# A chunked delta-rule and forgetting-attention block: the filling projections of its last stage as pairs of 64-row products

## What is computed

```python
h = rmsnorm(x, norm_w)                       # 1024 tokens x 1024
proj = h @ w_in                              # gdn q/k/v/z/beta/alpha, fox q/k/v/z/f, 2048 gate logits
y_a = gated_deltanet(...)                    # 8 heads of 64, chunks of 64
y_b = forgetting_attention(...)              # 8 heads of 64, 128-query blocks:
#   s = q k^T / 8 + c_t - c_s  (s <= t);  softmax(s) @ v;  rmsnorm, times silu(z)
g_a, g_b = split(sigmoid(gate_logit + gate_b))
merged = g_a * (y_a @ w_up_gdn) + g_b * (y_b @ w_up_fox)
out = rmsnorm(x + merged @ w_out)
```

## Time and profile before

| | us |
|---|---|
| median of 3 runs | 946.38 (946.35 to 946.46) |
| the profiled execution | 946.32 |
| its span, first to last instruction | 944.5 |
| TensorE busy | 924.9 (98%) |
| VectorE busy | 610.3 (65%) |
| ScalarE busy | 473.1 (50%) |

### The profile page before, as it was taken

The page is one execution under the profiler, slowest core; times in us unless marked ns, Lnnn a source line. Parts: engine busy times, 40 slices in busy tenths (PEclk is TensorE's granted clock), DMA queues, the critical chain, the costliest instruction groups (busy, mean ns, idle before and its releaser), DMA issues.

```text
span 944.5 us, 15969 instructions
## 1 busy us (share of the span) xinstructions
PE 924.9 (98%) x6404; PEld 702.3 (74%) x6404; DVE 610.3 (65%) x983; ACT 473.1 (50%) x846; POOL 19.9 (2%) x29
## 2 busy tenths in 40 slices
PE   5999999999999999999999999999999999999997
PEld 5778787888888876676766666666667888888886
DVE  6487668799999934464496786767863433246252
ACT  7555654632866625532756547556554442334132
POOL 1000002020000000000000000000000000000000
PEclk9999999999999999999999999999999999999999
DMA  7111351249323393322553325234125323123162
GB/s 249 47 49 45 98 177 48 69 145 229 96 90 106 107 272 87 102 75 90 139 182 98 105 101 168 102 101 123 34 69 178 113 66 90 55 112 112 41 192 79
DMA packets 114704, 104.87 MB, mean 111 GB/s; under 512 B 33152, under 2 KB 94720, under 8 KB 114248
## 3 DMA queue, kind: packets, MB, share of 16 engines
q1 hardware_dynamic: 103256, 81.05, 30.4%
q10 hardware_dynamic: 10224, 18.62, 5.3%
q0 software_dynamic: 1152, 4.19, 1.4%
HBM read 76.84 MB, written 27.00 MB: 110 GB/s over the span
## 4 chain that ended last, share of the span: by engine, by line
PE 45%; DVE 3%; ACT 1%; DMA 1%; issue 1%; SPq 0%; DVEq 0%; ACTq 0%
PE pj L2287 6%; PE pj L2289 5%; PE pj L2288 5%; PE pc L2420 4%; PE pa L2386 3%; PE pa L2355 1%; PE pj L2298 1%; PE pj L2299 1%; PE pj L2300 1%; PE pj L2558 1%; PE pj L2556 1%; PE pj L2557 1%; PE pb L2446 1%; PE pb L2435 1%; PE pb L2557 1%; PE pb L2556 1%
## 5 line engine op out<-in xcount | busy, mean ns | idle before, releaser
L145 PE MATMUL pj<-h_hi,w_hi 128*128 128x512 f32 x504 | 203.6, 404 | 0.5 <-DVE w_lo L133 0.5
L146 PE MATMUL pj<-h_lo,w_hi 128*128 128x512 f32 x504 | 196.9, 391 | 0.0
L147 PE MATMUL pj<-h_hi,w_lo 128*128 128x512 f32 x504 | 196.5, 390 | 0.0
L145 PEld LDWEIGHTS pj<-h_hi,w_hi 128*128 128x128 f32 x504 | 94.5, 188 | 23.9 <-issue 1.1
L147 PEld LDWEIGHTS pj<-h_hi,w_lo 128*128 128x128 f32 x504 | 94.6, 188 | 20.4
L146 PEld LDWEIGHTS pj<-h_lo,w_hi 128*128 128x128 f32 x504 | 94.7, 188 | 17.9 <-issue 0.2
L2287 PE MATMUL pj<-h_hi,w_hi 128*128 128x512 f32 x248 | 101.3, 408 | 0.3 <-PEq L323 0.3
L2289 PE MATMUL pj<-h_hi,w_lo 128*128 128x512 f32 x248 | 96.8, 390 | 0.0
L2288 PE MATMUL pj<-h_lo,w_hi 128*128 128x512 f32 x248 | 96.7, 390 | 0.0
L2287 PEld LDWEIGHTS pj<-h_hi,w_hi 128*128 128x128 f32 x248 | 46.5, 188 | 19.5 <-issue 10.1
L598 ACT ACTIVATE xc<-pj 128x512 f32<-128x512 f32 x39 | 23.3, 597 | 72.2 <-PE pj L147 71.6
(11 more groups left out here) (372 smaller groups left out, 1867.9 us busy)
## 6 DMA issues: line engine op xcount, KB each, us to landing
w_raw<-in_w_in SPq DMA_DIRECT2D x48, 512.0 KB, 4.4
fox_scratch<-xc ACTq DMA_DIRECT2D x39, 256.0 KB, 2.8
qkv<-in_x SPq DMA_DIRECT2D x8, 512.0 KB, 6.4
fa<-rows_scratch POOLq DMA_DIRECT2D x8, 512.0 KB, 4.9
rv<-fr_scratch SPq DMA_DIRECT2D x16, 256.0 KB, 4.0
ma<-m_scratch SPq DMA_DIRECT2D x8, 512.0 KB, 3.9
rv<-in_w_out SPq DMA_DIRECT2D x8, 512.0 KB, 3.6
w_raw<-in_x SPq DMA_DIRECT2D x8, 512.0 KB, 4.4
```

The source lines that it names most:

```text
L145: nc.tensor.matmul(o, w_hi[:, slot, k], h_hi[:, k, cols], start=(k == 0), stop=False)
L146: nc.tensor.matmul(o, w_hi[:, slot, k], h_lo[:, k, cols], start=False, stop=False)
L147: last = nc.tensor.matmul(o, w_lo[:, slot, k], h_hi[:, k, cols], start=False, stop=(k == KT - 1))
```

## The change

From the second part of tile 1 on, the fills of tiles 1 to 7 are no longer products of 128 rows. `both_halves` gives TensorE each product as two of 64 rows, one for each half of the contraction rows, at the same time for different token halves: rows 0 to 63 add to half 0's bank while rows 64 to 127 add to half 1's (phase 0), and in phase 1 the other way round. `phase_done` holds phase 1 back until the banks of phase 0 are written. A fill is now a group of 24 such products (`fill()`), ten for each pair of heads, at the steps in `GROUP_STEP`: four groups for a gate tile, two for its up projection.

So both halves of a tile end at the same time. Both banks of `pj` hold gates and then both hold ups; there is a second pair of buffers `gate_r` and `mst_r`, and the up weights have one buffer for tiles 0 to 8. The two exponentials of a tile stand behind each other at one step, the two `plus` and `sigmoid` at the next. The first gate group of a tile waits for both `gated` of the tile before, the first up group for both exponentials. `gated` moves ahead in VectorE's steps. The up weights of tile 1, which were loaded beside tile 0's and split before the loop, are loaded and split at its start; the gate of tile 1's second half, still of 128 rows, is the first filling. Tile 9's up weights are split one round later.

```diff
-        up_hi = sb("up_hi", [P, 2, PAIRS, P], F32R, where=st)
-        up_lo = sb("up_lo", [P, 2, PAIRS, P], F32R, where=st)
+        up_hi_a = sb("up_hi_a", [P, PAIRS, P], F32R, where=st)
+        up_lo_a = sb("up_lo_a", [P, PAIRS, P], F32R, where=st)
+        with ExitStack() as own_gates:
+            gate_r = sb("gate_r", [P, HALF], where=own_gates)
+            mst_r = sb("mst_r", [P, HALF], where=own_gates)
+        up_hi_b = sb("up_hi_b", [P, PAIRS, P], F32R, where=st)
+        up_lo_b = sb("up_lo_b", [P, PAIRS, P], F32R, where=st)
...
-        gate_b1, mst_b1 = fa[:, 5, 0:HALF], fa[:, 6, 0:HALF]
+        gate_of, mst_of = (gate[:, :], gate_r[:, :]), (mst[:, :], mst_r[:, :])
+        up_hi = lambda tile: (up_hi_b if tile > KT and tile % 2 else up_hi_a)[:, :, :]
+        up_lo = lambda tile: (up_lo_b if tile > KT and tile % 2 else up_lo_a)[:, :, :]
...
-        AHEAD = 32
-        FILLS = ((8,) + (4,) * 4 + (0, 4) * 4) * PAIRS + (5, 4, 4, 3)
-        UNIT = KT + PAIRS
-        A_FILLS = KT * 2 * UNIT
+        GROUPS = 10
+        GROUP_STEP = (0, 0, 1, 2, 3, 4, 6, 8, 10, 12)
+        GATE_END = [None, 1] + [7 + 6 * t for t in range(KT - 2)]
+        UP_END = [None, 3] + [9 + 6 * t for t in range(KT - 2)]
...
-                    if tile > 1:
+                    if tile:
                         sp.wait_ge(up_ready, tile)
                     col = (tile % KT) * P
                     for b in range(2):
                         to = half_rows(1 - b if tile < KT else b)
-                        sp.dma_start((up_side if tile == 1 else up_raw)[to],
-                                     up_view[tile // KT][half_rows(b), :, col:col + P]).then_inc(
-                                         ma_loaded[0] if tile == 1 else up_loaded, 16)
+                        sp.dma_start(up_raw[to], up_view[tile // KT][half_rows(b), :, col:col + P]).then_inc(up_loaded, 16)
...
-                load_up(1)
...
-                load_up(2)
+                load_up(1)
                 for g in range(STEPS + TAIL):
                     p, s = divmod(g, PER)
                     v = s - 1
@@ -1563,6 +1558,8 @@
                     if v == 0 and p:
                         sp.wait_ge(u_step, 4 * p - 1)
                         load_fox(fz, 3, p, fz_loaded)
+                    if g == 1:
+                        load_up(2)
...
-                    if tile == 1:
-                        act.wait_ge(ma_loaded[0], SIDE)
-                    else:
-                        act.wait_ge(up_loaded, 32 * max(tile, 1))
-                    if tile >= 2:
+                    act.wait_ge(up_loaded, 32 * tile + 32)
+                    if 1 <= tile <= KT:
+                        act.wait_ge(up_done, 2 * tile)
+                    elif tile == KT + 1:
+                        act.wait_ge(up_free, 2 * KT)
+                        act.wait_ge(m_stored, 16 * 2 * KT)
+                    elif tile:
                         act.wait_ge(up_done, 2 * (tile - 1))
-                    nc.scalar.activation(up_hi[:, tile % 2], up_source(tile), ACT.Copy).then_inc(up_hi_done, 1)
+                    nc.scalar.activation(up_hi(tile), up_raw[:, :, :], ACT.Copy).then_inc(up_hi_done, 1)
...
-                    act.wait_ge(up_free, 1 if v == 2 else v)
-                    gate_exp(v, pj[:, 0], gate[:, :])
+                    if v >= 2:
+                        act.wait_ge(up_free, v - 1 if v < 4 else 2 * (v // 2))
+                    gate_exp(v, pj[:, v % 2], gate_of[v % 2])
...
                 exp_a(2)
+                split_up_hi(1)
                 store_m(1)
...
-                        split_up_hi(t + 2)
+                        split_up_hi(t + 1)
                     for u in gates_through(g):
                         exp_a(u)
...
-                def gated(v, buf, dst):
+                def gated(v):
                     dve.wait_ge(gate_act, 2 * v + 2)
-                    dve.wait_ge(up_done, v + 1)
+                    dve.wait_ge(up_done, 2 * (v // 2) + 2 if v >= 2 else v + 1)
                     if v == 0:
                         dve.wait_ge(const_made, 6)
-                    if v != 1:
-                        dve.wait_ge(m_stored, 16 * v)
-                    nc.vector.tensor_tensor(dst, pv_bank if v == 1 else pj[:, 1], buf, ALU.mult).then_inc(up_free, 1)
+                    if v >= 2:
+                        dve.wait_ge(m_stored, 16 * 2 * (v // 2))
+                    up = (pj[:, 1], pv_bank)[v] if v < 2 else pj[:, v % 2]
+                    nc.vector.tensor_tensor(mst_of[v % 2], up, gate_of[v % 2], ALU.mult).then_inc(up_free, 1)
...
-                split_up_lo(1)
...
-                        split_up_lo(t + 2)
+                        split_up_lo(t + 1)
...
-                        gated_steps(g)
                     elif s == 0:
                         if p:
                             low_part(p, 0)
                         row_max(p, 0)
                         if p == 0:
-                            gated(1, gate_b1, mst_b1)
+                            gated(1)
+                            split_up_lo(1)
                         row_max(p, 1)
                         row_max(p, 2)
                         row_max(p, 3)
                         low_part(p, 1)
-                        gated_steps(g)
                         spread_max(p, 0)
                         plus_steps(g)
                         gate_steps(g)
                     elif v < 4:
                         if v < 2:
                             row_max(p, 4 + 2 * v)
+                        if v > 1:
+                            add_weights(p, v - 1)
+                        gated_steps(g)
                         if v < 3:
                             plus_steps(g)
-                        if v > 1:
-                            add_weights(p, v - 1)
                         row_max(p, 5 + 2 * v)
                         if v == 3:
                             plus_steps(g)
@@ -2141,7 +2139,6 @@
                             out_gate(p - 1, 1)
                             add_squares(2 * p - 1)
                         gate_steps(g)
...
+                def both_halves(w, src, k, phase, first, last, done_sem, turns):
+
+                    for m, (w_part, s_part) in enumerate(((w[0], src[0]), (w[0], src[1]), (w[1], src[0]))):
+                        for r in range(2):
+                            half = r ^ phase
+                            ins = nc.tensor.matmul(pj[:, half], w_part[half_rows(r)], s_part[half_rows(r), k, half_cols(half)],
+                                                   start=(first and m == 0), stop=(last and m == 2))
+                            if last and m == 2:
+                                ins.then_inc(done_sem, 1)
+                            if turns and m == 2:
+                                ins.then_inc(phase_done, 1)
+
+                def gate_group(tile, c):
+
+                    slot = (N3 + tile) % 2
+                    if c == 0:
+                        pe.wait_ge(w_ready, N3 + tile + 1)
+                        pe.wait_ge(up_free, 2 * tile)
+                    phase = c // 2
+                    if c == 2:
+                        pe.wait_ge(phase_done, 4 * tile - 4)
+                    for k in range(4 * (c % 2), 4 * (c % 2) + 4):
+                        both_halves((w_hi[:, slot, k], w_lo[:, slot, k]), (h_hi, h_lo), k, phase,
+                                    phase == 0 and k == 0, phase == 1 and k == KT - 1, pj_done, phase == 0 and k == KT - 1)
+
+                def up_group(tile, phase):
+
+                    if phase == 0:
+                        pe.wait_ge(up_ready, tile + 1)
+                        pe.wait_ge(pj_free, 2 * N3 + 2 * tile + 4)
+                    else:
+                        pe.wait_ge(phase_done, 4 * tile - 2)
+                    for k in range(PAIRS):
+                        both_halves((up_hi(tile)[:, k], up_lo(tile)[:, k]), (ya_hi, ya_lo), k, phase,
+                                    phase == 0 and k == 0, phase == 1 and k == PAIRS - 1, up_done, phase == 0 and k == PAIRS - 1)
+
+                def fill():
+
+                    n = done[0]
+                    done[0] += 1
+                    if n < 2:
+                        for k in range(4 * n, 4 * n + 4):
+                            gate_product(3, k)
+                    elif n < 4:
+                        up_group(1, n - 2)
+                    else:
+                        tile, c = 2 + (n - 4) // 6, (n - 4) % 6
+                        if c < 4:
+                            gate_group(tile, c)
+                        else:
+                            up_group(tile, c - 4)
...
                         weight_sums(p - 1, 1)
                     max_scores(p, 0)
                     max_scores(p, 1)
-                    fill(3)
+                    fill()
                     max_scores(p, 2)
                     turn_values(p, 0)
                     max_scores(p, 3)
-                    fill(5)
+                    fill()
```

118 lines of the change are left out of this document (49 added, 69 removed).

## The result

The changed kernel takes 962.8 us, median of four runs (962.1 to 963.5), against 946.4 us of the kernel before, run beside it (four runs, 946.35 to 948.75). The ratio is 1.0163, with a 95% interval of 1.0146 to 1.0179. It is slower, as forecast, by 16.4 us where 11.7 were expected. The profiled execution took 963.3 us, with a span of 961.5.

What follows compares the result with a forecast made beforehand. TensorE, busy 924.9 of 944.5 us at full clock, was taken as the bound. 946.32 - 7.4 (shape changes) + 1.6 (pairs) + 10.2 (start waits) + 7.3 (later waits) = 958.0 us; forecast 954 to 962, range 946 to 964.

Steps and rivals of the forecast that it cites:

- rival 3: More waits of the later kind, 1.5 to 2 us for each of seven tiles: 12 instead of 7.3, time 963; chance 0.07.
- (c): Pair 0, step 1: ScalarE must split tile 3's late-loaded gate weights before slot 1's exponentials; TensorE's piece 8 waits 4.0 us.
- TensorE's own row: 39 fewer changes of shape at 0.19 us save 7.4 us, 456 pairs add 1.6: 5.8 us won.
- (a): Start of pair 0: VectorE's split of tile 1's late-loaded up weights delays piece 3 by 4.1 us, `turn_max` by 0.7.
- (b): Start of pair 0: exponential of tile 1's second half stands behind a sigmoid and weight split on ScalarE; 1.4 us.
- Tiles 4 and 5's gates: First gate groups in pairs 1 and 2 wait for both `gated` of the tile before: 1.85 and 2.1 us.
- step 9: Pairs 0 and 3: two sigmoids and a weight split ahead of slot 9's exponentials delay slot 11's scores, 0.65 us each.
- Slot 7 of pair 2: Two sigmoids and a weight split go ahead of slot 5's exponentials, whose bank slot 7 needs: TensorE waits 2.15 us.
- 1 (absorbed): Other engines run ahead enough to absorb the waits; only TensorE's own terms remain: 940.5 us; chance 0.12.
- Rival 2: Only the start's waits come; the five later ones vanish as each lets other engines catch up: 950.7 us; chance 0.18.
- Rivals 4 and 5: 4: pairs not side by side, over 1000 us, chance 0.02; 5: an added product costs 0.025 us, 967.8 us, chance 0.03.

Runs made afterwards that it cites:

- e8_full_rows: e6_all_exp with its fills run as products of 128 rows again, order on the other engines kept: 948.6 us (1.0026 to the kernel before).
- e4_later: The changed kernel with only the later waits mended by reordering VectorE and ScalarE, start left as is: 956.3 us (1.0101 to the kernel before).
- e6_all_exp: e5_all with the exponential of tile 1's second half ahead of the sigmoid and weight split in pair 0's step 0: 943.2 us (0.9966 to the kernel before).
- e5_all: The changed kernel with the edits of e3_start and e4_later, and tile 7's gate weights split one step later: 945.4 us (0.9990 to the kernel before).
- e1_up_early: The changed kernel with the load of tile 1's up weights issued earlier by SP: 957.1 us (1.0108 to the kernel before).
- b1_up_late: The kernel before, products of 128 rows, with tile 1's up weights loaded and split late, tiles 2 and 3 split some steps later: 953.6 us (1.0083).
- e3_start: The changed kernel with tile 1's up weights loaded early and tile 3's gate weights split one step later: 953.5 us (1.0071 to the kernel before).
- e7_all_no27: e6_all_exp with the gated products of tile 4 back behind the first row maximum of pair 2's step 1: 945.0 us (0.9983 to the kernel before).
- e2_w3_late: The changed kernel with ScalarE splitting tile 3's gate weights one step later, behind slot 1's exponentials: 959.2 us (1.0130 to the kernel before).

## Why the prediction was right, and where it was not

The direction and the mechanism were right. TensorE saves its changes of shape and meets more waits than that is worth. The forecast of 958.0 us is 4.8 below the measured time. The stated range, 946 to 964, takes that in, but the forecast's own 954 to 962 does not: its upper end was set for rival 3 and for a late landing in (c), and neither happened. That 962.8 lies inside is luck. Step by step:

- **TensorE's own row.** -5.8 forecast, -5.2 by `e8_full_rows`, -4.9 by the table. The number of changes and their 0.19 us held. The 1.6 us for 456 pairs were not there (a pair costs no more than a product), but neither was all of the 7.4: by `e8_full_rows` some 1.9 are lost at waits and short of them.
- **(a), (b), (c).** 4.8, 1.4 and 4.0 forecast, 4.8, 1.3 and 3.3 in the trace, and three edits that each take one away give back 5.8, 2.2 and 3.6 us, with what the clock does. That (a) hit its sum is partly luck: 4.1 us were meant for piece 3 and 0.7 for `turn_max` behind it, and the trace has 4.8 at piece 3 and none at `turn_max`, which now follows a fill at 1.2 GHz that takes 2.1 us longer. (c) was over-sized by 0.7: ScalarE's load landed in 3.9 us instead of 4.4, and TensorE came later than assumed. (Its range, 3.2 to 5.5 "by the landing", does not follow from its own 3.6 to 6.5 us, which would have given 3.2 to 6.1.)
- **Tiles 4 and 5's gates, step 9.** 5.25 forecast, 5.0 found.
- **Slot 7 of pair 2.** 2.15 forecast, 0.6 found. That ScalarE's doubled step makes TensorE wait is right, but not for what: not slot 7's scores for a bank, but `weight_sums` for the row norms, 0.36 us here and 1.49 in `e4_later`. In the changed kernel another wait stood some 6 us ahead of it and covered most of it.
- **That other wait was missed.** The forecast looked at every reader of `gated` and of the exponentials, but not at `split_up_lo`, of which it said nothing after tile 1. It cost 1.9 us.
- **The step that failed is the sum.** It took TensorE's durations of the kernel before for all of its row, "busy at the full clock", while adding waits of 4 us which that kernel does not have. Three fills ran at 1.2 GHz and cost 5.1 us more. That is the miss: the profiled execution, for which the sum was made, took 963.3, 5.3 above it, and the other errors (+0.9 for TensorE's row, -0.8 for the start, +0.5 for the later waits, -0.5 ahead of them) cancel, by chance.

Of the rivals, 1 (absorbed) is what `e6_all_exp` had to be made for: 943.2 us against its 940.5, but only with another order on three engines. Rival 2, that each wait lets the others catch up, holds at one place, the step of slot 7. Rival 3's time (963) is what was measured, for another reason: the later waits came to 7.8 us, not 12. Rivals 4 and 5 are refuted by the distance of the pairs; that a pair costs what one product costs is `e8_full_rows`' answer too. The Trainium skill's overhead for each matmul (TensorEngine Tiling, Instruction Overhead), which the prediction turned into an estimate of 11.4 us, does not show as a price of the second product of a pair: ten pairs take 2.28 us and ten products 2.27.

What stays open is why the clock falls after one wait and not after another of the same length, or after the same wait in one execution and not in another, and where the spread of `e5_all` comes from. The traces are one execution for each kernel, so the count of stretches at 1.2 GHz is that execution's.

## What to carry to other kernels

A saving on the bounding engine that hands twice the work to the others at once is a gain only if the load, the split and the reader of that work are put where there is slack; here the same products gave +16.4 us in one order and -3.4 us in another (of which 5.2 are the products' own and the order costs 2.0). For every operand of a moved step, ask what reads it first and when it can be loaded, also for those that the change does not name. And where a change makes TensorE wait for over a microsecond, price the work that follows at the lower clock as well: the fill behind a wait of 1.4 us took 4.40 us in `e4_later` and 2.81 in `e6_all_exp`, depending on whether the clock fell.

## What the runs showed of the hardware

- TensorE's granted clock fell to 1.2 GHz at every wait of over 3 us in these traces, seven of seven, from 3.15 us (`e1_up_early`, 497.5) to 5.97 (`b1_up_late`, 479.6), for 3.4 or 6.8 us. At waits of 1.2 to 1.9 us it fell in some traces and not in others: not behind the 1.87 us of the changed kernel at 582.5, but behind the same wait in `e3_start` (571.7); behind 1.37 us in `e4_later` (620.2), not behind 1.36 us in `e6_all_exp`. And it differs between executions of one kernel: the mean granted clock of `e7_all_no27` is 0.999 in four executions and 0.997 or 0.998 in six. A fill in such a stretch cost 1.4 to 2.1 us more.
- The Trainium skill (TensorE: Matmul & The Clock Gate, What's actually happening) says that the clock is at its lower level when the engine has been idle, and the rows of the long waits agree. They add that a wait of 1.2 us in otherwise busy work can come right before the fall (`e2_w3_late`, 495.2).
- A change of tile shape cost 0.19 us, and two products of 64 rows side by side took 0.228 us, as one of 128 rows.
